# Placing the matmul operand tiles of a two-layer decoder trunk at multiples of 2048 bytes

## The reference

```python
def conformer_conv_module(x, w_in, b_in, w_dw, b_dw, ln_g, ln_b, w_out, b_out):
    h = x @ w_in + b_in
    a, gate = jnp.split(h, 2, axis=-1)
    h = a * jax.nn.sigmoid(gate)
    h = causal_depthwise_conv(h, w_dw, b_dw)          # 31 taps
    h = jax.nn.silu(layer_norm(h, ln_g, ln_b))
    return h @ w_out + b_out

def conv_ffn(x, w_up, b_up, w_dw, b_dw, w_down, b_down):
    h = x @ w_up + b_up                                # 1024 -> 2 * 2816
    h = causal_depthwise_conv(h, w_dw, b_dw)           # 3 taps
    g, val = jnp.split(h, 2, axis=-1)
    return (jax.nn.silu(g) * val) @ w_down + b_down    # 2816 -> 1024

for i in range(2):
    y = conformer_conv_module(...) if i == 0 else chunked_spatial_gating(...)
    x = layer_norm(DEEPNORM_ALPHA * x + y, norm1_g[i], norm1_b[i])
    y = conv_ffn(x, ...)
    x = layer_norm(DEEPNORM_ALPHA * x + y, norm2_g[i], norm2_b[i])
```

## Time and profile before

| | |
|---|---|
| median of 3 runs | 1121.97 us (1120.92 to 1122.23) |
| profiled execution, first to last instruction (span) | 1119.3 us |
| PE busy | 1099.3 us, 98% of the span, 5069 matmuls |
| PEld busy | 909.4 us, 81% |
| DVE busy | 729.2 us, 65% |
| ACT busy | 435.4 us, 39% |
| mean granted TensorE clock | 0.994 |
| HBM | 98 GB/s over the span |

### The profile page before, as it was taken

One profiled execution on the slowest core, in us unless ns is written; L12 is line 12 of the kernel. 1 busy time (PEld: TensorE's weight loads), 2 busy tenths in 40 slices (PEclk: granted clock), 3 DMA queues, 4 the chain that ended last, 5 costly groups with the idle time before them and its releaser, 6 DMA issues.

```text
span 1119.3 us, 14443 instructions
## 1 busy us (share of the span) xinstructions
PE 1099.3 (98%) x5069; PEld 909.4 (81%) x5069; DVE 729.2 (65%) x970; ACT 435.4 (39%) x697; POOL 48.3 (4%) x58
## 2 busy tenths in 40 slices
PE   8799999999999999999999999999999999999997
PEld 6688887898888888888888888888888888888885
DVE  6999987669767676732336685677767677652325
ACT  7556563434334343421124243234434344331111
POOL 0800000000000000000000020010000000000001
PEclk9899999999999999999999999999999999999999
DMA  9212111403232332342233423311323232342211
GB/s 355 72 38 76 38 57 40 137 32 97 91 112 79 108 95 92 109 171 91 94 118 103 179 84 105 123 48 57 105 101 98 90 112 76 112 150 94 94 38 76
DMA packets 30999, 110.50 MB, mean 99 GB/s; under 512 B 3440, under 2 KB 3440, under 8 KB 30960
## 3 DMA queue, kind: packets, MB, share of 16 engines
q1 hardware_dynamic: 28944, 102.63, 27.4%
q10 hardware_dynamic: 2016, 7.34, 1.8%
HBM read 107.86 MB, written 2.10 MB: 98 GB/s over the span
## 4 chain that ended last, share of the span: by engine, by line
PE 95%; DVE 3%; DMA 1%; issue 0%; ACT 0%; SPq 0%; POOL 0%; DVEq 0%; POOLq 0%; ACTq 0%
PE ps L931 18%; PE ps L929 18%; PE ps L930 18%; PE ps L939 11%; PE ps L940 11%; PE ps L941 11%; PE ps L1005 2%; DVE acc L683 2%; PE ps L1006 2%; PE ps L1007 2%; PE ps L1067 1%; DVE wl L622 1%; DMA xraw<-d_x_fm 1%; PE ps L1133 0%; PE ps L1134 0%
## 5 line engine op out<-in xcount | busy, mean ns | idle before, releaser
L929 PE MATMUL ps<-xh,wh 128*128 128x512 f32 x832 | 324.3, 390 | 2.3 <-DVE xl L638 1.8
L931 PE MATMUL ps<-xh,wl 128*128 128x512 f32 x832 | 323.8, 389 | 0.0
L930 PE MATMUL ps<-xl,wh 128*128 128x512 f32 x832 | 323.7, 389 | 0.0
L622 DVE TENSOR_TENSOR wl<-raw,wh 128x1024 fp32r<-128x1024 f32 x86 | 107.4, 1252 | 174.5 <-ACT wh L384 174.5
L929 PEld LDWEIGHTS ps<-xh,wh 128*128 128x128 f32 x832 | 156.2, 188 | 36.6 <-DVE xl L638 2.4
L930 PEld LDWEIGHTS ps<-xl,wh 128*128 128x128 f32 x832 | 156.2, 188 | 32.4
L931 PEld LDWEIGHTS ps<-xh,wl 128*128 128x128 f32 x832 | 156.2, 188 | 32.4
L384 ACT ACTIVATE wh<-raw 128x1024 fp32r<-128x1024 f32 x86 | 90.4, 1054 | 183.8 <-PE ps L941 176.8
L939 PE MATMUL ps<-wh,hh 128*128 128x512 f32 x352 | 139.2, 395 | 0.0
L940 PE MATMUL ps<-wl,hh 128*128 128x512 f32 x352 | 139.0, 395 | 0.0
L941 PE MATMUL ps<-wh,hl 128*128 128x512 f32 x352 | 139.0, 395 | 0.0
(11 more groups left out here) (124 smaller groups left out, 1361.6 us busy)
## 6 DMA issues: line engine op xcount, KB each, us to landing
raw<-d_weights SPq DMA_DIRECT2D x180, 512.0 KB, 3.4
xraw<-d_x_fm SPq DMA_DIRECT2D x8, 256.0 KB, 6.3
res<-d_x_tm SPq DMA_DIRECT2D x4, 512.0 KB, 8.2
brow<-d_rows ACTq DMA_DIRECT2D x3, 512.0 KB, 4.0
grow<-d_rows ACTq DMA_DIRECT2D x3, 512.0 KB, 6.6
brow_n<-d_rows ACTq DMA_DIRECT2D x3, 512.0 KB, 8.3
d_out<-res SPq DMA_DIRECT2D x3, 512.0 KB, 2.6
brow<-d_rows SPq DMA_DIRECT2D x1, 512.0 KB, 9.8
```

Of the source, the lines that this page charges most:

```text
L622: eng.tensor_tensor(l, raw[:, u % RAW, :], h.bitcast(f32), ALU.subtract).then_inc(w_lo, 1)
L929: eng.matmul(ps[:, bank, cols], a, xh[:, k, cols], start=(k == 0), stop=False)
L930: eng.matmul(ps[:, bank, cols], a, xl[:, k, cols], start=False, stop=False)
L931: mm = eng.matmul(ps[:, bank, cols], b, xh[:, k, cols], start=False, stop=(k == KD - 1))
```

## The change

`place` rounds each size up to 64 bytes in place of 32. The small tiles (`ident` to `sqs`) are placed first. Two lines round the running offset up to a multiple of 2048, one ahead of `raw`, one at `h0`. No instruction is added, removed or moved on any engine: the built programs have the same rows in the same order. Only addresses differ. The whole diff:

```diff
@@ -33,6 +33,8 @@
 UNIT = 1024
+LINE = 64
+ROW = 2048
@@ -99,17 +101,9 @@
         if offset is None:
             offset = at[0]
-            at[0] += (size + 31) // 32 * 32
+            at[0] += (size + LINE - 1) // LINE * LINE
         return nc.alloc_sbuf_tensor_at(name, shape, dt, offset=offset)
 
-    raw = place("raw", [P, RAW, UNIT], f32)
-    wh = place("wh", [P, RING, UNIT], f32r)
-    wl = place("wl", [P, RING, UNIT], f32r)
-    xh = place("xh", [P, KD, SEQ], f32r)
-    xl = place("xl", [P, KD, SEQ], f32r)
-    res = place("res", [P, NT, D], f32)
-    par = place("par", [P, NPAR], f32)
-    brow = place("brow", [P, D], f32)
     ident = place("ident", [P, P], f32)
     half_m = place("half_m", [P, NT], f32)
@@ -120,6 +114,16 @@
     sqs = place("sqs", [P, NT], f32)
+    at[0] = (at[0] + ROW - 1) // ROW * ROW
+    raw = place("raw", [P, RAW, UNIT], f32)
+    wh = place("wh", [P, RING, UNIT], f32r)
+    wl = place("wl", [P, RING, UNIT], f32r)
+    xh = place("xh", [P, KD, SEQ], f32r)
+    xl = place("xl", [P, KD, SEQ], f32r)
+    res = place("res", [P, NT, D], f32)
+    par = place("par", [P, NPAR], f32)
+    brow = place("brow", [P, D], f32)
+
 
 
     s0 = at[0]
```

## The result

The changed kernel takes 1111.92 us (median of 4 runs, 1110.66 to 1112.87) against 1121.45 us for the kernel before in the same comparison (4 runs, 1118.44 to 1122.23): a ratio of 0.9922, 95% interval 0.9907 to 0.9936. By the ratio that is 8.7 us less (the two medians differ by 9.5); 9.3 were forecast, and 1112.7 us. Run again as e0_change, beside e5_taps_track, the change gave 0.9938 (0.9924 to 0.9952).

A forecast was written before the change was run, and what follows sets the result against it. The prediction took PE as the bound: number of matmuls times the distance between their starts. Its terms, 7.0 + 0.95 + 0.3 + 1.0, made about 9.3 us, taking the median from 1121.97 to 1112.7 us, range 1109.5 to 1116.0.

The forecast's parts named there:

- The room of 1.5 us at the transposes: Between a normalized block's last DVE operation and PE's transposes of it: over 1.5 us, so faster PE products need not wait.
- Term 1: 1056 down products from `hh` and `hl`: 6.6 ns less each, 7.0 us gained.
- Term 2: 144 down products with `eh`, `el` or `bh`, `bl` moving: 6.6 ns less each, 0.95 us gained.
- Term 3: 48 up products over all 512 tokens with `eh`, `el` stationary: 6.6 ns less each, 0.3 us gained.
- Term 4: 288 up products over 256 tokens: 116.7 to 113.3 ns each, 1.0 us gained, between no gain and 1.9 us.
- Term 5: Convolution taps, 236 counted: residues stay mixed, so 0, within 1.6 us gained or lost.
- Terms 6 to 8: Low-clock taps; spatial products, transposes, ACT and DVE operations; wider rounding, which costs memory only: no time gained or lost.
- The cause: Up and down products: an operand starting 32 bytes off a multiple of 64 costs 6.6 ns a matmul, 233.3 against 226.7.
- The rule on lines of 16 bytes: SBUF operand reads: only crossing a 16-byte line costs, so the sum would be 0 and the time 1121.97 us.
- Rows of 2048 bytes: Rival: 512-column moving slices pay for crossing a multiple of 2048; without crossings 213.3 ns steps, 1057 us; chance 0.06.
- Region: Rival: long steps come from tiles' place on the partition, above 135,000 bytes, not the residue; time stays 1121.97 us; chance 0.08.
- Collision: Rival: weight loads starting at the moving stream's residue delay it; 2928 products go to 233.3 ns, 1141 us; chance 0.04.

The follow-up runs named there:

- e0_change: The changed kernel run again unaltered, in a later comparison against the kernel before: 1111.88 us, ratio 0.9938.
- e5_taps_track: The changed kernel with each tap's diagonal tile starting as many bytes past a multiple of 256 as its moving slice: 1112.37 us, ratio 0.9931 to the kernel before.
- m2_streams: Trunk left out; the kernel's own up, down and 256-column up streams, weight tiles shifted by 0 to 1024 bytes: at 0, steps of 226.8, 226.7 and 119.9 ns.
- e2_all_32: The changed kernel with all operands of the up and down products 32 bytes further: 1113.36 us, ratio 0.9943 to the kernel before.
- e3_h_64: The changed kernel with `h0` 64 bytes further, so `hh`, `eh`, `bh` and their low tiles move, `wh` and `xh` not: ratio 0.9991 to the kernel before.
- e4_h_128: The changed kernel with `h0` 128 bytes further, every operand still on a multiple of 64: ratio 0.9999 to the kernel before.
- m1_residues: Trunk left out; groups of 16 equal matmuls for pairs of moving and stationary starting offsets: 229.4 ns at 64 and 0, 226.9 at 96 and 96.
- e1_line64: The kernel before with tile order kept, sizes and `h0` rounded up to 64 bytes, nothing to 2048: ratio 0.9935 to the kernel before.
- e6_eh_64: The changed kernel with `eh` and `el` 64 bytes further, `hh`, `hl`, `bh`, `bl` unmoved: 1113.41 us, ratio 0.9934 to the kernel before.

## Why the prediction was right, and where not

- *What bounds it*: right. Every us came from the distance between starts on PE, nothing from a wait, and nothing was caught up elsewhere. The room of 1.5 us at the transposes held: the block's last DVE operation ends at 595.48 us, and PE's transposes stand on the chain from 597.12 on.
- *Term 1*, 7.0 us from `hh` and `hl`: -6.98. *Term 2*, 0.95 us: -0.61 and -0.28, so 0.89. *Term 3*, 0.3 us: 0.26.
- *Term 4*, the 256-column products, is the step that failed. It said a gain of 1.0 us, between 1.9 and no gain; they became 0.89 us slower, 119.8 ns in place of 116.7. The lower end, "no gain", was set with no row to exclude a loss. The value was scaled from 512 columns, as if both widths followed the same rule; m2_streams shows that at distance 0 one is at its shortest and the other at its longest. This is 1.9 us of the sum.
- *Term 5*, the taps at 0: +0.06, with single steps as mixed as before. *Terms 6 to 8* at nothing: right.
- The sum of -9.3 us would have come to -7.2 by the streams. The times' own -8.7 has an interval from -7.2 to -10.4, with one at its edge and the other inside. That the median, 1111.92 us, came within 1 us of the forecast 1112.7 is therefore in part luck: the runs' spread hides the 1.9 us.
- *The cause*, "wherever one of the two operands starts 32 bytes off a multiple of 64": wrong in its generality. In the kernel before each such case also stood 32 bytes from a multiple of 256 away from its partner, and the rows couldn't tell the two readings apart. e2_all_32, e3_h_64 and e4_h_128 do. The forecast came out because it rested on a second ground, that afterwards the operands stand to each other as `xh` and `wh` did in the earlier trace rows. By the stated cause alone e3_h_64 would have won as much, and it won nothing clear of the spread: that rounding to 2048 also made every distance of the up and down products a multiple of 256 was luck as far as the stated cause goes.
- *The rule on lines of 16 bytes* (the Trainium skill: SBUF — State Buffer, Specifications) was set aside by the two levels at offsets that are multiples of 16, rightly, as a rule that would leave the time unchanged. But something with 16 bytes is there: in m1_residues and e5_taps_track the steps rank by the moving operand's start modulo 16.
- *Rows of 2048 bytes*: excluded, up products stayed at 226.7 ns though they no longer cross one, and e1_line64 needs none. *Region*: excluded, since `hh` got its short step at practically the same place. *Collision*: not at equal starts, at least for 512 columns, where those are the best ones; for 256 columns they are among the worst.

**What stays open** is what in the chip takes the extra 13 to 20 ns. At the low clock it isn't there (426.7 ns), it depends on how far apart the two operands start, with a sign, and a stream needs several matmuls to find its level. That would fit two readers that meet in the same memory, but this is argued and not shown, and so is which ones. The one attempt at it, fewer stationary columns, spoke against the simplest form: the extra time stayed, and only its dependence on the placement went. Open too are what chooses between two levels at the same addresses (e6_eh_64), and so whether the levels of single groups of m1_residues belong to the pair or to what ran before it.

## What to carry to other kernels

If TensorE is the bound and never idle, read the distance between the starts of matmuls by stream, not the duration: two levels for the same shape are a sign of placement. Then put the stationary and moving tiles of 512-column float32r products (128 stationary columns) a multiple of 256 bytes apart; here this was worth 6.6 ns of 233 on every such matmul that wasn't so placed, and rounding both to a larger number is only the simple way to get it. Bound an edit for each shape by itself, in both directions: what helps 512 columns cost 3 ns on 256, and on 384 the 32 bytes made no difference.

## What the runs showed of the hardware that was not expected

- The step of a 512-column float32r stream depends on the distance of its two operands modulo 256 bytes: 226.7 ns at 0; 229 where the moving one begins 64 bytes later; 232 to 234 at the other multiples of 32. Where it begins 16 bytes earlier, three of four pairs held 227 ns too. At 0, 32, 64 and 96 both operands can be shifted together without a loss; at 16 they can't (233 ns).
- 256-column streams are at their longest, 120 ns, at distance 0, lie between 116.6 and 120 at most other multiples of 32, and settled at 113.3 ns for some pairs of m1_residues (moving at 16 and stationary at 0, for one). The same addresses settled at 113.3 ns in e3_h_64 and at 117.7 in e6_eh_64.
- At distance 0 the settled step is 226.7 ns for 512 columns, 173.3 for 384 and 120.0 for 256. Less the columns at 2.4 GHz (213.3, 160.0 and 106.7 ns, scaled from the 426.7 ns at half the clock) that leaves 13.3 to 13.4 ns at each width. With 384 columns 32 bytes of distance changed nothing.
- A stream doesn't have its step at once. It wanders, in the streams looked at, for up to some ten matmuls and then mostly repeats a short pattern of steps. The pattern comes back in kernels laid out differently: of the 1055 steps of the down products from `hh` and `hl`, 1043 are equal to the nanosecond in the changed kernel and e1_line64, and all to within one.
- At the low granted clock (1.2 GHz) none of this shows: 426.7 ns is 512 columns exactly, also for badly placed taps.
